# Norm boundaries in token halves: two tiles of a feed-forward and four of a projection run half by half, the sums share one bank, and two of the next stage's four first units follow the norm

## The reference, cut to what matters

```python
def first_block(x, ...):
    h = x
    for i in range(DEPTH):                       # 2
        hn = rms_norm(h, norm_mix[i])
        mix = even_mixer(hn, ...) if i % 2 == 0 else odd_mixer(hn, ...)
        h = h + mix
        h = h + swiglu(rms_norm(h, norm_ffn[i]), ffn_gate[i], ffn_up[i], ffn_down[i])
    return rms_norm(h, norm_final)

def second_block(x, ...):
    for l in range(DEPTH):                       # 2
        x = layer_norm(ALPHA * x + 0.5 * swiglu_2(x, ...), ...)
        y = mlstm_mixer(x, ...) if l % 2 == 0 else window_attention(x, ...)
        x = layer_norm(ALPHA * x + y, ...)
        x = layer_norm(ALPHA * x + 0.5 * swiglu_2(x, ...), ...)
    return x
```

## Time and profile before

| what | value |
|---|---|
| median of three runs | 4340.07 us (4335.52 to 4343.68) |
| the profiled execution's own time | 4341.47 us |
| its span | 4339.6 us |
| PE busy | 3873.5 us (89%) |
| DVE busy | 2154.8 us (50%) |
| ACT busy | 1239.4 us (29%) |
| granted TensorE clock, mean | 0.907 |

### The profile page before, as it was taken

One profiled execution on the slowest core, in us unless ns is written; L12 is line 12 of the kernel. 1 busy time (PEld: TensorE's weight loads), 2 busy tenths in 40 slices (PEclk: granted clock), 3 DMA queues, 4 the chain that ended last, 5 costly groups with the idle time before them and its releaser, 6 DMA issues.

```text
span 4339.6 us, 43087 instructions
## 1 busy us (share of the span) xinstructions
PE 3873.5 (89%) x17308; PEld 2994.1 (69%) x17308; DVE 2154.8 (50%) x3241; ACT 1239.4 (29%) x2115; POOL 210.6 (5%) x399
## 2 busy tenths in 40 slices
PE   7988998999885559999999897699999999999997
PEld 5645745888751138888888764488888888568886
DVE  7444624643568866434443725364345435336434
ACT  3231222322231113223322322032223224433222
POOL 0000000000057600000000000000000000000000
PEclk9868967999976669999999988599999999999999
DMA  2201200223210002232323220022322232002221
GB/s 101 69 1 60 83 0 25 93 97 102 89 52 0 0 15 88 97 101 80 112 97 107 70 68 0 3 77 97 100 94 90 96 105 85 15 20 78 97 98 68
DMA packets 88634, 296.42 MB, mean 68 GB/s; under 512 B 15534, under 2 KB 16948, under 8 KB 88436
## 3 DMA queue, kind: packets, MB, share of 16 engines
q1 hardware_dynamic: 79844, 289.56, 19.9%
q10 hardware_dynamic: 8592, 4.12, 0.4%
HBM read 291.54 MB, written 2.10 MB: 68 GB/s over the span
## 4 chain that ended last, share of the span: by engine, by line
PE 72%; DVE 16%; ACT 3%; issue 1%; DMA 0%; ACTq 0%; DVEq 0%
PE ps L304 20%; PE ps L305 20%; PE ps L306 20%; PE ps L301 13%; DVE XT L632 1%; DVE WL L292 1%; DVE RS L677 1%; DVE VA L675 1%; DVE VA L676 1%; DVE od_w L1763 1%; DVE XT L634 1%; DVE od_w L1764 1%; ACT XH L503 0%; ACT wa_pt L2002 0%; ACT R L501 0%
## 5 line engine op out<-in xcount | busy, mean ns | idle before, releaser
L304 PE MATMUL ps<-XH,WH 128*128 128x512 f32 (+1 forms) x3376 | 1258.4, 373 | 85.5 <-DVE XL L640 52.4
L305 PE MATMUL ps<-XL,WH 128*128 128x512 f32 (+1 forms) x3376 | 1242.8, 368 | 0.0
L306 PE MATMUL ps<-XH,WL 128*128 128x512 f32 (+1 forms) x3376 | 1241.9, 368 | 0.0
L292 DVE TENSOR_TENSOR WL<-RAW,WH 128x1024 fp32r<-128x1024 f32 x548 | 665.0, 1230 | 315.5 <-ACT WH L286 309.2
L304 PEld LDWEIGHTS ps<-XH,WH 128*128 128x128 f32 x3376 | 653.5, 194 | 202.7 <-issue 53.3
L305 PEld LDWEIGHTS ps<-XL,WH 128*128 128x128 f32 x3376 | 654.0, 194 | 102.3 <-issue 3.4
L306 PEld LDWEIGHTS ps<-XH,WL 128*128 128x128 f32 x3376 | 653.2, 193 | 100.8
L286 ACT ACTIVATE WH<-RAW 128x1024 fp32r<-128x1024 f32 x548 | 565.4, 1048 | 127.1 <-PE ps L301 81.0
L304 PE MATMUL ps<-HH,WH 128*128 128x512 f32 (+1 forms) x1188 | 435.2, 366 | 0.0
L305 PE MATMUL ps<-HL,WH 128*128 128x512 f32 (+1 forms) x1188 | 434.1, 365 | 0.0
L306 PE MATMUL ps<-HH,WL 128*128 128x512 f32 (+1 forms) x1188 | 434.1, 365 | 0.0
(11 more groups left out here) (555 smaller groups left out, 3780.4 us busy)
## 6 DMA issues: line engine op xcount, KB each, us to landing
RAW<-units SPq DMA_DIRECT2D x548, 512.0 KB, 3.3
XIN<-in_x ACTq DMA_DIRECT2D x2, 1024.0 KB, 6.4
out<-OUT SPq DMA_DIRECT2D x4, 512.0 KB, 2.7
da_pi<-in_positions ACTq DMA_DIRECT2D x1, 256.0 KB, 3.9
od_pi<-in_positions ACTq DMA_DIRECT2D x1, 256.0 KB
wa_dist<-constants ACTq DMA_DIRECT2D x1, 192.0 KB, 2.3
da_lb<-in_ev_lambdas ACTq DMA_DIRECT2D x1, 128.0 KB, 3.6
od_bin<-in_od_b_re ACTq DMA_DIRECT2D x1, 128.0 KB
```

The source lines that it names most:

```text
L292: nc.vector.tensor_tensor(WL[:, u % RING, :], RAW[:, u % RING, :], WH[:, u % RING, :].bitcast(F32), ALU.subtract)\
L304: nc.tensor.matmul(out, wh, xh, start=start, stop=False)
L305: nc.tensor.matmul(out, wh, xl, start=False, stop=False)
L306: return nc.tensor.matmul(out, wl, xh, start=False, stop=stop)
```

## The change

A feed-forward computes its last two output tiles in halves, a mixer's output projection its last four (ev_attn, whose projection is not followed by a norm, none). The order stays: all halves 0, then the halves 1 with the sums of half 0 inside the first of them. Because tiles 6 and 7 of a feed-forward hold all six slots of the ring until their second half, no unit of the next stage is split before the norm; behind a mixer and the load two are. A table HI_AT now says how many units of the next stage are split after which step of the norm, for ScalarE and VectorE alike: unit 0 after step 3, unit 1 after step 5, units 2 and 3 after step 7, unit 4 after step 10, unit 5 after step 13; what has been split before is skipped. At step 2 VectorE finishes all half-1 tiles but the last, and the last at step 7, ahead of the splits of step 7 and `chain(1)`. first_units waits for units 0 and 1, goes k by k with two units, makes the sums of half 1 after the last k, then runs units 2 and 3 on half 0 and all four on half 1. Both sums lie in bank 5, S1 in its first and S2 in its second half, and OUT_BANK is in another order.

```diff
-        TAIL = dict(load=8, ffn=1, ev_attn=0, ev_mamba=3, od=3, win=3, mlstm=3)
+        TAIL = dict(load=8, ffn=2, ev_attn=0, ev_mamba=4, od=4, win=4, mlstm=4)
...
-            for u in range(3):
+            for u in range(2):
                 pe.wait_ge(S["split_ready"], n0 + u + 1)
             for k in range(KD):
                 pe.wait_ge(S["x_ready"], x0 + k + 1)
-                for u in range(3):
+                for u in range(2):
                     half(u, k, HALVES[0])
-                if k == 4:
-                    stats_pe(pe, nrm, 1)
-            pe.wait_ge(S["split_ready"], n0 + 4)
-            for k in range(KD):
-                half(3, k, HALVES[0])
+            stats_pe(pe, nrm, 1)
+            for u in range(2, 4):
+                pe.wait_ge(S["split_ready"], n0 + u + 1)
+                for k in range(KD):
+                    half(u, k, HALVES[0])
...
             if nrm["ln"]:
-                mm(ps[:, 4, hs], ones[:], S1[:, hs], True, False)
-                mm(ps[:, 4, hs], ones[:], R[:, KD - 1, hs], False, True)
-            mm(ps[:, 5, hs], ones[:], S2[:, hs], True, False)
-            mm(ps[:, 5, hs], ones[:], SQ[:, 1, hs], False, True).then_inc(S["stats_ready"], 1)
+                mm(ps[:, 5, HALVES[0]], ones[:], S1[:, hs], True, False)
+                mm(ps[:, 5, HALVES[0]], ones[:], R[:, KD - 1, hs], False, True)
+            mm(ps[:, 5, HALVES[1]], ones[:], S2[:, hs], True, False)
+            mm(ps[:, 5, HALVES[1]], ones[:], SQ[:, 1, hs], False, True).then_inc(S["stats_ready"], 1)
...
-            for m in range(KD - 1):
+            for m in range(KD - 2):
...
-            pe.wait_ge(S["r_ready"], e["r0"] + KD - 2)
-            down(KD - 1, ps[:, 7, HALVES[0]], HALVES[0], False).then_inc(S["tail_done"], 1)
-            pe.wait_ge(S["r_ready"], e["r0"] + KD - 1)
-            down(KD - 1, ps[:, 6, HALVES[1]], HALVES[1], True, lambda: stats_pe(pe, e["norm"], 0))
+            for q in range(KD - 2, KD + 2):
+                m, h = e["tiles"][q]
+                pe.wait_ge(S["r_ready"], e["r0"] + q - 1)
+                last = down(m, ps[:, 6 + m % 2, HALVES[h]], HALVES[h], h == 1,
+                            (lambda: stats_pe(pe, e["norm"], 0)) if q == KD else None)
+                if h == 0:
+                    last.then_inc(S["tail_done"], 1)
...
                 square_act(act, e, q)
-                hi_to(act, min(n + 3, n - 3 * KD + 3 * q + 8 if e["kind"] == "ffn" else n - KD + q + 5))
-            hi_to(act, n + 3)
+                if e["kind"] == "ffn":
+                    hi_to(act, min(n, n - 3 * KD + 3 * q + 8))
+                else:
+                    hi_to(act, min(n + 2, n - KD + q + 5))
...
                     if t == 3:
-                        for q in range(KD, KD + prod["tail"]):
+                        for q in range(KD, KD + prod["tail"] - 1):
                             square_act(act, prod, q)
-                    if t == 7 and final:
-                        outs(0, 4)
-                    if t in (5, 10, 13):
-                        hi_to(act, nx + {5: 4, 10: 5, 13: 6}[t])
+                    if t == 7:
+                        square_act(act, prod, KD + prod["tail"] - 1)
+                        if final:
+                            outs(0, 4)
+                    if t in HI_AT:
+                        hi_to(act, nx + HI_AT[t])
...
+            def ffn_tail(e, a, z):
+                for q in range(a, z):
+                    m, h = e["tiles"][q]
...
+                    finish(e, q, ps[:, 6 + m % 2, HALVES[h]], e["alpha"])
+                    if q == KD - 2:
+                        lo_to(dve, e["n1"])
...
                     if t == 2:
-                        second.get(e["prod"]["kind"], mixer_tail(1))(e["prod"])
-                    if t == 5:
-                        lo_to(dve, nx + 4)
+                        rest(prod, KD, KD + prod["tail"] - 1)
+                    if t == 7:
+                        rest(prod, KD + prod["tail"] - 1, KD + prod["tail"])
+                    if t in HI_AT:
+                        lo_to(dve, nx + HI_AT[t])
                     if t == 7:
                         chain(e, 1)
                         normed(8)
-                    if t in (10, 13):
-                        lo_to(dve, nx + {10: 5, 13: 6}[t])
...
-OUT_BANK = (4, 5, 0, 1, 2, 6, 7, 3)
+OUT_BANK = (5, 0, 1, 2, 4, 6, 7, 3)
+HI_AT = {3: 1, 5: 2, 7: 4, 10: 5, 13: 6}
```

More of the change, by code:

```diff
@@ L552, in finish @@
                     own(v.tensor_tensor(S2[:, hs], SQ[:, 0, hs] if m == 1 else S2[:, hs], SQ[:, m % 2, hs], ALU.add), "s2_added")
[L554 to L555 removed]
+            def ffn_tail(e, a, z):
+                for q in range(a, z):
+                    m, h = e["tiles"][q]
                     if h:
[L557 removed]
+                        dve.wait_ge(S["unit_done"], e["n1"] - 3 * (KD - 1 - m))
                     else:
[L559 to L561 removed]
@@ L563, in mixer_tail @@
-            def mixer_tail(h):
-                def go(e):
-                    for i in range(3):
-                        m = KD - 3 + i
-                        if h:
-                            dve.wait_ge(S["unit_done"], e["n1"] - 2 + i)
-                        else:
-                            dve.wait_ge(S["tail_done"], e["t0"] + i + 1)
-                        finish(e, m + 3 * h, ps[:, OUT_BANK[m], HALVES[h]], e["alpha"])
-                return go
-            def load_half(h):
-                def go(e):
-                    for q in range(8 * h, 8 * h + 8):
-                        dve.wait_ge(S["xt_ready"], q + 1)
-                        finish(e, q, ps[:, 6 + q % 2, 0:HT], None)
-                return go
@@ L581, in _, with mixer_tail @@
-            second = dict(load=load_half(1), ffn=ffn_tail(1))
+                        dve.wait_ge(S["tail_done"], e["t0"] + m - KD + 3)
+                    finish(e, q, ps[:, 6 + m % 2, HALVES[h]], e["alpha"])
+                    if q == KD - 2:
+                        lo_to(dve, e["n1"])
+            def mixer_tail(e, a, z):
+                for q in range(a, z):
+                    m, h = e["tiles"][q]
+                    if h:
+                        dve.wait_ge(S["unit_done"], e["n1"] - (KD - 1 - m))
+                    else:
+                        dve.wait_ge(S["tail_done"], e["t0"] + m - KD + 5)
+                    finish(e, q, ps[:, OUT_BANK[m], HALVES[h]], e["alpha"])
@@ L583, in load, with load_tiles @@
+            def load_tiles(e, a, z):
+                for q in range(a, z):
+                    dve.wait_ge(S["xt_ready"], q + 1)
+                    finish(e, q, ps[:, 6 + q % 2, 0:HT], None)
+            second = dict(load=load_tiles, ffn=ffn_tail)
             def load(e):
-                load_half(0)(e)
+                load_tiles(e, 0, KD)
                 dve.wait_ge(S["vec_ready"], 1)
@@ L587, in load @@
                     own(v.tensor_copy(VEC[:, a:b], ps[:, 0, a:b]), "vec_copied" if n + 1 == len(vec_pages()) else None)
-                lo_to(dve, 3)
+                lo_to(dve, 2)
             def ffn(e):
@@ L601, in ffn @@
                     lo_to(dve, n0 + 2 * j + 6)
-                for m in range(KD - 1):
+                for m in range(KD - 2):
                     dve.wait_ge(S["unit_done"], nd + 3 * m + 3)
                     finish(e, m, ps[:, 6 + m % 2, :], e["alpha"])
-                    lo_to(dve, min(e["n1"] + 3, nd + 3 * m + 8))
-                ffn_tail(0)(e)
-                lo_to(dve, e["n1"] + 3)
+                    lo_to(dve, min(e["n1"], nd + 3 * m + 8))
+                ffn_tail(e, KD - 2, KD)
             def chain(e, h):
-                hs = HALVES[h]
-                s1, s2, y, x, a = ps[:, 4, hs], ps[:, 5, hs], RS[:, h, :], VA[:, 0, :], VA[:, 1, :]
+                s1, s2, y, x, a = ps[:, 5, HALVES[0]], ps[:, 5, HALVES[1]], RS[:, h, :], VA[:, 0, :], VA[:, 1, :]
                 dve.wait_ge(S["stats_ready"], 2 * e["c"] + h + 1)
@@ L624, in norm @@
             def norm(e):
-                ln, final, nx = e["ln"], e["final"], e["next"]
+                ln, final, nx, prod = e["ln"], e["final"], e["next"], e["prod"]
+                rest = second.get(prod["kind"], mixer_tail)
                 def normed(t):
@@ L658, in norm @@
                         normed(8)
-                    if t in (10, 13):
-                        lo_to(dve, nx + {10: 5, 13: 6}[t])
             stages = dict(load=load, ffn=ffn, norm=norm,
-                          **{k: (lambda m: lambda e: m["dve"](dve, own, e, finish, mixer_tail(0)))(m) for k, m in mixers.items()})
+                          **{k: (lambda m: lambda e: m["dve"](dve, own, e, finish, mixer_tail))(m) for k, m in mixers.items()})
             for e in plan:
@@ L698, in outproj_pe @@
             if h == 1 and m == whole:
-                pe.wait_ge(S["r_ready"], e["r0"] + 2)
+                pe.wait_ge(S["r_ready"], e["r0"] + 1)
                 b["stats_pe"](pe, e["norm"], 0)
@@ L708, in outproj_dve @@
     if e["tail"]:
-        tail(e)
```

(3 more changed lines are left out.)

6 lines of the change are left out of this document (removed).

## The result

The changed kernel takes 4356.28 us (median of 5 runs, 4355.62 to 4359.66) where the kernel before takes 4340.07 (5 runs, 4335.52 to 4343.68): ratio 1.0041, 95% interval 1.0027 to 1.0056. It is 16.2 us slower; the forecast was 8.6 slower with a range that ended at 4356. The profiled execution took 4357.8, span 4356.0, against a span of 4339.6 before: 16.4 to explain.

The account below looks back on a forecast made before the run. TensorE bounds the kernel, idling at norms for VectorE's chains. Terms 3 x 1.9 + 2 x 1.0 + 2 x 0.7 + 2 x 0.8 - 3.5 + 1.4 = +8.6 us gave 4348.7; own range 4343 to 4355, stated range 4339 to 4356.

Parts of the forecast that it names:

- Bound, and what the change can reach: Whole kernel: TensorE is the bound; its 100 us idle at the eleven norms is all the change can reach.
- Half tiles cost more: Extra half-width matmuls on TensorE: 0.86 us in each of six feed-forwards, 0.31 in each of four mixers, 6.4 in all.
- Splits of the weights: Feed-forward boundaries: splits 0 and 1 behind norm steps 3 and 5 delay TensorE to 21.8 us; gap 4.3 becomes 7.1.
- Layer-norm boundaries: Norms with a layer norm: +1.9 us behind each of three feed-forwards, +0.7 behind each of two mixers.
- RMS feed-forwards: Two RMS norms behind feed-forwards, ahead of od and f00: gap 2.5 for 2.0, second chain some 8 us later, +1.0 each.
- Load and store: First and last boundary: load +1.4 us (0 to +3), store -3.5 (-4.6 to -2.6).
- One bank: Sums in one bank, outputs in others: costs nothing; at most 0.46 us a norm, 5 us, if reading and writing met.
- the clock at some 15 gaps: Uncertainty at gaps: the clock falls or not at each, 1.7 to 2.2 us, together -5 to +4.
- The clock that pays back: Rival: no low clock at longer first gaps saves 8 us in all, end near 4341; chance 0.12.
- Free splits: Rival: second chain starts by 25.1 us after the sums, not held by splits; 39 less, about 4310, half 4330; chance 0.09.
- Late weights: Rival: part 2 of tile 7 split 2.4 us late in each of five feed-forwards, 12 more, 4361; chance 0.09.
- A wait elsewhere: Rival: another wait decides, as the constants' DMAs ahead of od; no change to the sum; no chance given.

Follow-up runs that it names:

- second pair of profiles: The changed kernel and the kernel before, both unedited and profiled again: 4355.4 us (ratio 1.0038) and 4344.0 us.
- the run with the fill: Changed kernel with six unread matmuls of 512 columns in TensorE's wait ahead of the window mixer's first scores: 4343.9 us, ratio 1.0009.
- the better places alone: Kernel before with unit 3's high part behind ScalarE's step 1, its subtraction behind VectorE's step 6, last two splits one step apart: 4330.4 us, ratio 0.9977.
- both together: Changed kernel with split tables of their own for ScalarE and VectorE, by kind of preceding stage: 4310.4 us, ratio 0.9939 (with six filler matmuls 4312.2).

## Why the prediction was wrong

**Bound, and what the change can reach.** The bound is right: TensorE idles at the norms as much as before, 102.7 us for 100. "All that the change can reach" is wrong: most of what it did to the time happened in a mixer, where TensorE is busy at half the clock.

**Half tiles cost more.** The 492 matmuls are there: 17800 for 17308. A feed-forward's sums come 7.04 us earlier and not 7.92, so a half tile pair costs what the rows said, 0.013 us. The formula of the Trainium skill (TensorE: Matmul & The Clock Gate, Back-to-back issue gap) gives an estimate of 7.75, which the trace does not bear out.

**Splits of the weights.** Right to 0.1 us in its starting time (21.8), and shown to be the cause by moving them: the gap went from 6.95 to 2.60.

**Layer-norm boundaries.** +1.9 against 2.1, 1.4 and 2.3; mixers +0.7 against 0.7 and 0.7. Right. (In the second pair of profiles 1.4, 1.7, 2.4 and 0.7, 0.8.) The differences among the three are the clock: behind the same 6.9 us gap the low level ended 24.9 us after the sums at one and 26.7 and 26.8 at the other two, whose second sums came 0.8 later.

**RMS feed-forwards.** +1.0 each against 0.1 and 2.5: right in the sum (2.0 against 2.5), wrong in both. At f00 the second chain came 9.5 us later (2046.06 from 2019.52, before 17.0 from the sums) and not "some 8": the gap was 3.08, not 2.5, and 6.8 us at the low clock followed it. In the second profile they were 3.4 us, the chain came 8.2 later and the boundary was +1.2, so most of the miss at f00 is that execution's clock. At od's the clock did not fall at all, in both.

**Load and store.** +2.1 for +1.4, within its bounds; the second pair has -0.5, outside them: this boundary differs by 1.5 us between two executions of the changed kernel (46.5 and 45.0 us) and by 1.2 between two of the kernel before. Store -2.2 for -3.5, outside the bounds given (-4.6 to -2.6): the second chain came 21.8 after the sums, just past the upper end of 19.7 to 21.7, since the sums went at the low clock (chain 3.9 us behind them, the end of the 1.9 to 3.9 that I had allowed):

```profile
4330.12 1.19 PE L301 MATMUL ps<-S,ones 128*128 128x256 f32 x2 [3.12 <-ACT SQ L403]
...
4333.98 0.43 DVE L618 TENSOR_SCALAR VA<-ps 128x256 f32<-128x256 f32 x1 [4.03 <-PE ps L301]
```

**One bank.** Nothing, as taken: the steps of the chain are 0.46 apart as before.

**The step that failed** is one that the prediction never wrote down: its sum ran over the norms, and took the mixers between them as unchanged but for the half tile, a term of nothing without a reason. The range had "the clock at some 15 gaps", each 1.7 to 2.2 us, all of them at norms. The window mixer has one wait of 1.4 us in it; at the place to which the change put it, the clock fell behind it and stayed low for 27 us, 11.4 us of time. It was shown three ways: filled, it goes; shifted by 1.1 us, it goes; shifted by 2.0 us in the kernel before, it comes. Had the scores fallen elsewhere, the same change would have measured near 4345 (4356.3 less 11.4; the run with the fill has 4343.9, ratio 1.0009), inside the range and within 4 us of the forecast. So the miss is this one term, and a hit would have been partly luck as well: the stages that I took at nothing were 5.3 us shorter in this profile, which I had not foreseen either.

**The rivals.** The clock that pays back: only at od's boundary (+0.1 for +1.0); elsewhere it took. The Trainium skill's advice that I had cited beside it (avoid idle gaps between bursts of matmuls; TensorE: Matmul & The Clock Gate, Why this matters for your kernels) is about longer gaps than the one that decided. I had applied it to the gaps that the change made longer; the wait of 1.39 us, which it only moved, was followed by 27.3 us at the low clock. Free splits: no; the second chain starts at 28.5 and 30.9, not by 25.1. Late weights: no such wait among those ahead of the tail matmuls. A wait elsewhere: the constants' DMAs ahead of od do decide there, and TensorE waits 9.4 us for them behind its first units, for 9.8 before; this changed nothing.

## What to carry to other kernels

When work is put behind a reduction to cover its latency, ask what the added work displaces: here the ring slots of the next weights, whose splits then stood in the very gap that was to be filled. Cover and preparation have to be moved together, each engine's part at a step of its own; the longer halves alone made this kernel 16 us slower (11 of them by the clock in the window mixer), the better places alone 10 us faster, both together 30.

When a kernel is bound by an engine whose clock depends on what it did before, list every wait on it, also those in stages that the change doesn't touch, and put into the range what a fall of the clock behind each would cost. A difference of 10 us in an untouched stage that comes back in each execution is not noise, and need not be the change's mechanism; a few filler matmuls at the wait, or a shift by 1 to 2 us, told it here. And look at all times of a run, not at the median alone: two groups 11 us apart can hide in it.

## What the hardware showed that I had not expected

- A wait of 1.39 us can be followed by 27.3 us at the low clock, through matmuls that follow each other nearly without a break (clock 0.50, TensorE busy 26.8 of 27.3 us), or by none, as the place of the wait differs by 1 to 2 us. Moved by 0, 2.0 and 6.35 us in the kernel before, it gave no, the whole and no stretch.
- It repeated in the two profiles of the changed kernel: 269.37 and 269.38 us. The mlstm mixer varies by 5 us between the same two. And ten executions of the kernel with the feed-forward part undone fall into two groups about 11 us apart; no profile shows the slower group, so whether it has the stretch is open.
- Six matmuls of 512 columns that nobody reads, in that wait, took 11.5 to 12.4 us off the kernel (its two measurements), and 12.7 off the window mixer.
